# A two-block transformer kernel: another order in the first stage, in cross attention, in the queue of weight loads, and one bank given back earlier

## The reference, cut to what matters

```python
# first block
h = x
proj = rmsnorm(h, g_mix) @ w_in                     # rq rk rv rg fq fk fv ff
h = h + concat(silu(rg) * head_group_norm(retention(rq, rk, rv)),
               forgetting_attention(norm(fq), norm(fk), fv, ff)) @ w_out
h = h + memory_cross_attention(rmsnorm(h, g_xattn), mem, ...) @ w_xo
h = h + (silu(hn @ w_gate) * (hn @ w_up)) @ w_down  # hn = rmsnorm(h, g_ffn)
# memory_cross_attention: 4 heads of 256, 512 queries, 256 memory tokens
q = rmsnorm_per_head(hn @ w_xq); k = rmsnorm_per_head(kv[:half]); v = kv[half:]
o = softmax(q @ k.T / 16) @ v
# second block
mods = silu(c) @ w_ada + b_ada                      # 72 rows of 128 values
...                                                 # swiglu, convolution + window attention, swiglu
```

## Time and profile before

| | |
|---|---|
| median of 3 runs | 2117.18 us (2116.45 to 2119.18) |
| profiled execution: its own time | 2116.05 us |
| its span | 2114.2 us |
| TensorE busy | 2053.4 us (97%), 9844 matmuls |
| VectorE / ScalarE / GpSimd busy | 948.8 / 722.0 / 846.2 us |
| mean granted TensorE clock | 0.991 |

### The profile page before, as it was taken

How to read it: one execution, slowest core, us unless ns; L and a number is a source line. 1 busy time by engine, 2 the same in 40 slices (tenths; PEclk the granted TensorE clock), 3 DMA queues, 4 the chain that set the end, 5 groups by cost and what they waited for, 6 DMA issues and landing times.

```text
span 2114.2 us, 27008 instructions
## 1 busy us (share of the span) xinstructions
PE 2053.4 (97%) x9844; PEld 1685.6 (80%) x9844; DVE 948.8 (45%) x1247; ACT 722.0 (34%) x1092; POOL 846.2 (40%) x347
## 2 busy tenths in 40 slices
PE   7999899989999998999999999999999999999998
PEld 6787787868788877888888878888777888888886
DVE  3585864243888885432221143473543243222112
ACT  4234454243323322333222233224664343223221
POOL 3344323304454443344444434444223444444442
PEclk9999999999999999999999999999999999999998
DMA  5243212204556575223323324422222322323331
GB/s 198 80 130 119 81 61 73 87 11 140 179 189 197 190 266 200 91 90 99 94 94 100 97 83 119 132 97 90 67 64 70 99 90 90 99 92 97 100 95 64
DMA packets 66504, 233.26 MB, mean 110 GB/s; under 512 B 7552, under 2 KB 8832, under 8 KB 65920
## 3 DMA queue, kind: packets, MB, share of 16 engines
q1 hardware_dynamic: 64992, 229.54, 34.2%
q10 hardware_dynamic: 1440, 2.72, 0.4%
HBM read 224.37 MB, written 2.10 MB: 107 GB/s over the span
## 4 chain that ended last, share of the span: by engine, by line
issue 65%; POOL 29%; PE 5%; POOLq 1%; DVE 0%; ACT 0%; DVEq 0%
POOL wlo L414 29%; PE bank L1637 2%; PE bank L1639 2%; PE bank L1638 2%; POOLq L413 0%; POOLq L417 0%; DVE h L1498 0%; PE bank L1671 0%; DVE ssum L919 0%; POOLq L414 0%; PE bank L1662 0%; PE bank L1661 0%; DVE h L1016 0%; DVEq L123 0%; ACT tmp L494 0%
## 5 line engine op out<-in xcount | busy, mean ns | idle before, releaser
L414 POOL TENSOR_TENSOR wlo<-raw,whi 128x1024 fp32r<-128x1024 f32 x343 | 846.0, 2467 | 1245.3 <-ACT whi L440 1245.1
L1539 PE MATMUL bank<-xh,whi 128*128 128x512 f32 x1664 | 651.6, 392 | 2.3 <-ACT whi L440 1.1
L1540 PE MATMUL bank<-xl,whi 128*128 128x512 f32 x1664 | 647.7, 389 | 0.0
L440 ACT ACTIVATE whi<-raw 128x1024 fp32r<-128x1024 f32 x343 | 362.3, 1056 | 660.1 <-PE bank L1545 358.9
L1545 PE MATMUL bank<-xh,wlo 128*128 128x512 f32 x1664 | 411.2, 389 | 0.0
L1539 PEld LDWEIGHTS bank<-xh,whi 128*128 128x128 f32 x1664 | 312.4, 188 | 69.7 <-ACT whi L440 1.9
L1545 PEld LDWEIGHTS bank<-xh,wlo 128*128 128x128 f32 x1664 | 312.4, 188 | 65.1
L1540 PEld LDWEIGHTS bank<-xl,whi 128*128 128x128 f32 x1664 | 312.5, 188 | 64.3 <-issue 0.5
L1637 PE MATMUL bank<-hh,whi 128*128 (+1 forms) x528 | 206.9, 392 | 7.3 <-POOL wlo L414 7.2
L1638 PE MATMUL bank<-hl,whi 128*128 (+1 forms) x528 | 206.4, 391 | 0.0
L1639 PE MATMUL bank<-hh,wlo 128*128 (+1 forms) x528 | 206.3, 391 | 0.0
(11 more groups left out here) (273 smaller groups left out, 2157.0 us busy)
## 6 DMA issues: line engine op xcount, KB each, us to landing
raw<-units SPq DMA_DIRECT2D x343, 512.0 KB, 3.5
ada_w<-ada_rows SPq DMA_DIRECT2D x72, 512.0 KB, 4.5
h<-x_t SPq DMA_DIRECT2D x8, 256.0 KB, 6.7
dec<-decays ACTq DMA_DIRECT2D x8, 256.0 KB, 2.9
out_t<-h SPq DMA_DIRECT2D x8, 256.0 KB, 2.1
mem_in<-mem_t SPq DMA_DIRECT2D x1, 1024.0 KB, 12.7
turned_q<-proj SPq DMA_DIRECT2D x4, 256.0 KB, 5.7
turned_k<-proj SPq DMA_DIRECT2D x4, 256.0 KB, 4.1
```

The lines of the kernel that those rows point to most:

```text
L414: pool.tensor_tensor(wlo[:, j % 2 * UNIT:(j % 2 + 1) * UNIT], raw[:, j * UNIT:(j + 1) * UNIT], whi[:, j % 2 * UNIT:(j % 2 + 1) * UNIT].bit ...
L440: act.activation(whi[:, v % 2 * UNIT:(v % 2 + 1) * UNIT], raw[:, slot * UNIT:(slot + 1) * UNIT], ACT.Copy).then_inc(hi_ready, 1)
L1539: mm(bank[:, 0:n], wh, chunk(rhs[0], t, n), start=t == 0, stop=False)
L1540: mm(bank[:, 0:n], wh, chunk(rhs[1], t, n), start=False, stop=False)
```

## The change

First stage: x chunk 0 is loaded ahead of unit 0, and `csilu` moves from ACT's queue to the end of SP's first loads. ACT makes the high parts of x and units 0 and 1 first, and all squares after them; DVE makes all low parts, then itself the low parts of units 0 and 1, then the sums. POOL starts with unit 2. TensorE runs all high passes of the two units, the second two tiles behind the first, and then both low passes. Group norm: the root of the last variance goes to `xn` instead of back into bank 6, and TensorE waits for the root only. Cross attention: a second pair of banks for scores, the last `xq` unit cut around the scores of head 0, scores two heads ahead at the start, the second pair of norms between, and tiles of `xo` between the last heads. Rows: the last eight modulation rows come two units later.

```diff
-XAT_NORM_BANKS = (4, 5, 2, 5)
+XAT_NORM_BANKS = (4, 5, 0, 1)
+XAT_SCORE_BANKS = ((0, 1), (2, 5))
...
+            load_x((0,))
             load_unit(0, 0, True)
-            load_x((0, 1))
+            load_x((1, 2))
             load_unit(1, 1, True)
-            load_x(range(2, C))
+            load_x(range(3, C))
...
+            sp.dma_start(csilu[:, :], c_rows).then_inc(c_in, 16)
...
-                    if rows < (64 if u < half + 3 else NMOD * C):
+                    if rows < (64 if u < half + 5 else NMOD * C):
...
-            with pool.Fori(0, UNITS // 4) as i:
+            pool.wait_ge(lo_ready, 2)
+            for v in (2, 3):
+                low_part(v, v)
+            with pool.Fori(1, UNITS // 4) as i:
                 for j in range(4):
                     low_part(4 * i + j, j)
...
-            act.dma_start(csilu[:, :], c_rows).then_inc(c_in, 16)
+            def mix_high(c):
+                act.wait_ge(x_loaded[c], 16)
+                act.activation(chunk(xh, c), chunk(h, c), ACT.Copy, scale=col("g_mix", c)).then_inc(norm_hi, 1)
+            act.wait_ge(setup_done, 1)
+            act.activation(rs[0:32, 0:1], lt[0:32, 0:1].bitcast(f32), ACT.Copy)
+            act.wait_ge(vec_in, 16)
+            mix_high(0)
             high_part(0, 0, 0)
-            act.wait_ge(vec_in, 16)
+            mix_high(1)
+            mix_high(2)
+            high_part(0, 0, 1)
+            for c in range(3, C):
+                mix_high(c)
             for c in range(C):
-                act.wait_ge(x_loaded[c], 16)
-                norm_chunk("mix", c, c % 4, dst=xh, gain="g_mix")
-                if c == 0:
-                    high_part(0, 0, 1)
+                norm_chunk("mix", c, c % 4)
             high_part(0, 0, 2)
+            high_part(0, 0, 3)
             norm_root_of("mix")
-            high_part(0, 0, 3)
             norm_r_copy("mix")
...
-                act.activation(bank[:, :], bank[:, :], ACT.Sqrt, bias=col("eps")).then_inc(gn_root, 1)
+                if p == 3:
+                    act.wait_ge(gn_t, 3)
+                act.activation(bank[:, :] if p < 3 else chunk(xn, 0), bank[:, :], ACT.Sqrt, bias=col("eps")).then_inc(gn_root, 1)
...
                 act.wait_ge(qn_sum, pair + 1)
-                act.activation(qroot[:, 8 * pair:8 * pair + 8], banks[6 + pair][:, 0:8], ACT.Sqrt,
+                act.activation(qroot[:, 8 * pair:8 * pair + 8], banks[(6, 0)[pair]][:, 0:8], ACT.Sqrt,
                                bias=col("eps")).then_inc(qn_root, 1)
...
+            def memory_exps(hd):
+                act.wait_ge(xat.s_negmax, hd + 1)
+                if hd >= 2:
+                    act.wait_ge(xat.s_tr, hd - 1)
+                for q, b, o, w, po in XAT_GROUPS:
+                    act.activation(xat.p[hd % 2][:, po:po + w], banks[XAT_SCORE_BANKS[hd % 2][b]][:, o:o + w], ACT.Exp,
+                                   bias=nm[:, 4 * hd + q:4 * hd + q + 1], scale=xat.scale,
+                                   accum_out=sm[:, 4 * hd + q:4 * hd + q + 1]).then_inc(xat.s_exp, 1)
+            def memory_probabilities_copy(hd):
+                act.wait_ge(xat.s_tr, hd + 1)
+                if hd >= 1:
+                    act.wait_ge(xat.s_pv, hd)
+                act.activation(xat.pt[:, 0:T], banks[3][:, :], ACT.Copy).then_inc(xat.s_pt_act, 1)
+            def memory_out_high(hd):
                 act.wait_ge(xat.s_pv, hd + 1)
                 for d in range(2):
                     act.activation(chunk(yh, 2 * hd + d), banks[6 + d][:, :], ACT.Copy).then_inc(xat.s_hi, 1)
-            attention(xat, xat_evac, later_roots, copy_first=True)
+            query_squares(1, range(3), lambda c: (qn_sum, 1))
+            memory_exps(0)
+            query_squares(1, (3,), None)
+            high_part(L["xo"].u0, 0, 1)
+            memory_probabilities_copy(0)
+            memory_exps(1)
+            query_roots(1)
+            memory_out_high(0)
+            memory_probabilities_copy(1)
+            memory_exps(2)
+            memory_out_high(1)
+            memory_probabilities_copy(2)
+            memory_exps(3)
+            memory_out_high(2)
+            memory_probabilities_copy(3)
+            memory_out_high(3)
...
-                norm_chunk("mix", c, dst=(xh, xl), gain="g_mix")
+                low_chunk("mix", c, h, T, (xh, xl), "g_mix")
+            for u in range(2):
+                dve.wait_ge(hi_ready, u + 1)
+                tt(wlo[:, u * UNIT:(u + 1) * UNIT], raw[:, u * UNIT:(u + 1) * UNIT],
+                   whi[:, u * UNIT:(u + 1) * UNIT].bitcast(f32), ALU.subtract).then_inc(lo_ready, 1)
+            for c in range(C):
+                norm_chunk("mix", c)
...
-                dve.reciprocal(chunk(xn, 0), banks[5 if p < 2 else 6][:, :]).then_inc(gn_rstd, 1)
+                dve.reciprocal(chunk(xn, 0), chunk(xn, 0) if p == 3 else banks[5 if p < 2 else 6][:, :]).then_inc(gn_rstd, 1)
...
             scale_units("xq", lambda j: chunk(xq, j), last=5)
             query_square_sums(0)
             scale_units("xq", lambda j: chunk(xq, j), first=5, last=6)
             query_recips(0)
             scale_units("xq", lambda j: chunk(xq, j), first=6, last=7)
             query_norm(0)
+            query_norm(1)
+            query_square_sums(1, (0,))
+            memory_maxima(0)
             scale_units("xq", lambda j: chunk(xq, j), first=7)
-            query_norm(1)
-            query_square_sums(1)
-            def xat_evac(hd):
-                for d in range(2):
-                    c = 2 * hd + d
-                    dve.wait_ge(xat.s_hi, c + 1)
-                    tt(chunk(yl, c), banks[6 + d][:, :], chunk(yh, c).bitcast(f32), ALU.subtract).then_inc(xat.s_lo, 1)
-            attention(xat, None, xat_evac, later_recips, later_queries)
+            memory_normalise(0)
+            query_square_sums(1, (1,))
+            memory_probabilities_copy(0)
+            memory_maxima(1)
+            memory_normalise(1)
+            query_recips(1)
+            query_norm(2)
+            query_norm(3)
+            memory_probabilities_copy(1)
+            memory_out_low(0)
+            memory_maxima(2)
+            memory_normalise(2)
+            memory_out_low(1)
+            memory_maxima(3)
+            memory_probabilities_copy(2)
+            memory_normalise(3)
+            memory_probabilities_copy(3)
+            memory_out_low(2)
+            memory_out_low(3)
...
+            def opening_units():
+                for t in range(C + 2):
+                    for m, k in ((0, t), (1, t - 2)):
+                        if 0 <= k < C:
+                            if k == 0:
+                                take(m)
+                                pe.wait_ge(hi_ready, m + 1)
+                            pe.wait_ge(norm_lo, k + 1)
+                            high_passes(m, (k,), banks[m], X, T)
+                for m in range(2):
+                    pe.wait_ge(lo_ready, m + 1)
+                    low_pass(m, banks[m], X, T).then_inc(unit_used, 1)
+            opening_units()
             def wait_consts_then_columns():
                 pe.wait_ge(consts_in, 32)
                 norm_columns("mix")
-            dense("fq", [X], T, (sc, SCALED["fq"]), together=((norm_lo, 0), paced),
+            dense("fq", [X], T, (sc, SCALED["fq"]), begun=True,
...
-                    pe.wait_ge(gn_rstd, 4)
+                    pe.wait_ge(gn_root, 4)
...
+            def memory_scores(hd):
                 pe.wait_ge(qn_done, 2 * hd + 2)
                 for q, b, o, w, _ in XAT_GROUPS:
+                    b = XAT_SCORE_BANKS[hd % 2][b]
+                    if o == 0:
+                        take(b)
...
+                last.then_inc(xat.s_scores, 1)
+                for b in XAT_SCORE_BANKS[hd % 2]:
+                    bank_free[b] = [(xat.s_exp, 4 * hd + 4)]
...
+                pe.wait_ge(xat.s_pn, 4 * hd + 4)
+                take(3)
+                take(4)
...
+                pe.wait_ge(xat.s_pt_act, hd + 1)
+                pe.wait_ge(xat.s_pt_dve, hd + 1)
+                take(6)
+                take(7)
...
+                last.then_inc(xat.s_pv, 1)
+                bank_free[6] = bank_free[7] = [(xat.s_lo, 2 * hd + 2)]
...
+            dense("xq", [Y], T, (sc, SCALED["xq"]), together=((norm_lo, HI_BASE["xattn"]), sum(held(7), [])), hooks=hooks,
+                  hold_last=True)
+            last_query = L["xq"].u0 + C - 1
+            half_unit(last_query, last_query % 2, banks[3], Y, T, 0)
+            pe.wait_ge(kmem_done, C)
+            pe.wait_ge(vmem_copied, C)
+            memory_scores(0)
+            half_unit(last_query, last_query % 2, banks[3], Y, T, 1)
+            memory_scores(1)
+            memory_transposes(0)
+            query_columns(1)
+            memory_values(0)
+            query_spread(1)
+            memory_transposes(1)
+            memory_scores(2)
+            memory_values(1)
+            memory_scores(3)
+            memory_transposes(2)
```

(27 more changed lines are left out.)

86 lines of the change are left out of this document (42 added, 44 removed).

## The result

The changed kernel takes 2093.97 us in the median of four runs (2092.98 to 2095.66), the kernel before 2117.27 (2116.45 to 2119.18): a ratio of 0.9894 with a 95% interval of 0.9881 to 0.9906. Forecast were 2092.9 and a range of 2088.5 to 2101. The profiled execution took 2094.07, with a span of 2092.3.

A forecast was written before the change was run, and what follows sets the result against it. TensorE bounds the kernel, busy 2053.4 of 2114.2 us; idle and half-clock time can be won. Gains of 5.2 + 1.7 + 9.6 + 7.8 = 24.3 give 2092.9 us from the median of 2117.18; range 2088.5 to 2101.

The forecast's parts named there:

- First stage, forecast 5.2: First stage: it ends at 21.1 instead of 26.4, gain taken as 5.2 us; bounds 2.8 and 6.5.
- My cover of 1.8 us for the columns: First stage: DVE's six additions end at 19.3, under low passes that end at 21.1, so `norm_columns` need not wait.
- Group norm, forecast 1.7: Forgetting attention's first values: no longer behind DVE's reciprocal, the chain moves by 1.7 us; bounds 0.8 and 2.5.
- Cross attention, forecast 9.6: Cross attention: 5.5 us of waits, 2.8 of half clock and 1.3 of drained pipelines go; bounds 5.5 and 11.7.
- The step on the columns: Cross attention: columns wait 0.9 us for DVE's second sum, queued behind the normalisation and slowed beside POOL.
- eight places at 0.2: Cross attention: pipelines drained between stages, about 0.2 us at each of eight places that now run on, entered as 1.3.
- Rows, forecast 7.8: Down projection: the 5.4 us wait goes and 2.4 of half clock with it; bounds 5.0 and 8.2.
- such shifts: Whole kernel: other half-clock spells may shift the time by 2 us, allowed for in the range.
- A: Rival: the waits go but the clock still falls at all three places, 2100.5 us; chance 0.11.
- B: Rival: in cross attention one late step in ACT's and DVE's in-order queues delays the next head, 2098 us; chance 0.06.
- C: Rival: in the rows, unit 129 or 130 takes over the wait, half of 7.8 lost, 2097 us; chance 0.04.
- D: Rival, slower: cross attention's short groups with small waits keep the clock low, 2128 us; chance 0.02.

The follow-up runs named there:

- p_gn: The kernel before with only the group norm edit (last root out of its bank, into `xn`): 2112.91 us, ratio 0.9986.
- a_nocut: The changed kernel with the last `xq` unit run whole ahead of the scores of head 0, not cut around them: 2093.78 us.
- a_gn2: The changed kernel with DVE's last group norm reciprocal and its scaling one head later, the low part of pair 2 ahead of both: 2099.73 us in one run.
- a_rows4: The changed kernel with the last modulation rows one unit later than in the kernel before, instead of two: 2093.91 us.
- a_poollow: The changed kernel with POOL instead of DVE making the low parts of units 0 and 1: 2095.09 us, ratio 0.9902.
- a_fill: The changed kernel with three tiles of the next unit instead of one between columns and spread in two otherwise unedited norms: 2087.50 us, ratio 0.9866.

## Why the prediction was right, step by step

**First stage, forecast 5.2.** 5.37 against the profile of before, by the steps that were given: unit 0's high part made TensorE start at 6.86 (6.5), the second tile at 8.33 (7.9), DVE's low parts took 1.2 each, the low passes ended with the columns at once behind them at 21.06 (21.1). Three steps were off and fell out against each other. The clock rose after nine slow matmuls and not fifteen. The splits were later than counted, so the low parts were ready at 15.2 and 16.4 (14.0 and 15.2). And the sums did not run at 0.68: each addition waits in a semaphore for the one before it on DVE, 0.79 from start to start, and they began at 16.3, so they ended at 21.0 and not at 19.3. My cover of 1.8 us for the columns was 0.1. Against what before usually takes, the gain is smaller: the five profiles of the old stage lie at 0, 0.13, 1.04, 1.10 and 1.28, and the profile that I summed from was the most expensive; the seven of the new stage have a median of 5.37, so about 4.3.

**Group norm, forecast 1.7.** Right in mechanism, and in size against the profile of before: TensorE gained 2.56 at the first values and gave 0.82 back, with the wait that the earlier trace rows had made me expect at the next hand-over. But that profile happened to have no spell behind the wait of 3.05. Three of the five profiles of the old stage have one; against their median (-1.58 in the rest of forgetting attention) the gain is 3.4, as `p_gn` measured with 3.5. The sum had no term for that spell. In after, TensorE's timeline:

```profile
261.80 0.41 PE L2003 MATMUL bank<-tab,tmp 128*128 128x128 f32 x2 [1.04 <-DVE tmp L1368]
```

**Cross attention, forecast 9.6.** 9.58. The waits named last were there in size: the spread 0.88 (0.9), values 3 0.79 (0.7), values 2 0.10 (0.2). The clock was 1.00. The step on the columns failed: no wait of 0.9 came, since DVE's second sum was not held up by POOL. I had charged this one operation 2.6, what two took in rows 8. DVE in after:

```profile
418.59 0.68 DVE L1393 TENSOR_TENSOR tmp<-tmp 128x512 f32<-128x512 f32 x1
```

The size of the spread's wait is partly luck: TensorE was there 0.7 earlier than counted, having no wait at the columns, and DVE's chain 0.6 earlier, since it started from the end of the transposes and not from the late sum. The waits are so 1.8 and not 2.7, and the idle time fell by 6.4 instead of 5.5; that made up for a smaller gain in busy time, 3.2 instead of 4.1 (2.8 for the clock and 1.3 for the pipelines, where eight places at 0.2 would have been 1.6). Here too before's profile was dear: four other profiles of the old stage take -0.27, 0.97, 0.98 and 1.00 less, nearly all of it a shorter spell. Against their median of all five, 0.97, the gain is 8.6.

**Rows, forecast 7.8.** 8.15, with no wait from unit 127 to 131. What is queued behind SP's block of rows is unit 129, as foreseen. SP in after, the answer to the earlier trace rows:

```profile
787.31 11.22 SPq L308 DMA_DIRECT2D raw<-units  x3
810.77 1.60 SPq L320 DMA_DIRECT2D ada_w<-ada_rows  x2
...
812.40 0.43 SPq L308 DMA_DIRECT2D raw<-units  x1
```

The group of three holds units 126, 127 and 128, the last issued at 798.2; unit 129 goes out at 812.40. Counted in before's time (14.9 later) that is 827.3, where unit 127 stood.

**The sum.** 24.3 was forecast. The four places gave 24.8 (5.37 + 1.74 + 9.58 + 8.15), but the profiled executions are only 22.0 apart. What is missing lies outside the four steps, in spells: 1.67 lost ahead of the first values, 1.10 and 0.55 at the two norms, and 0.6 won at the end. I had put such shifts at 2 us in the range. Taken from medians of all profiles, the terms are 4.3 + 3.4 + 8.6 + 8.1 = 24.4, against 23.3 in the runs' medians, whose interval reaches from 19.9 to 25.2. So the sum of 24.3 is good to a us, but by luck in part: the first stage and cross attention are worth 0.9 and 1.0 less than I forecast, since before's profile was dear there, and the group norm 1.7 more, since it was cheap there.

**The rivals.** A did not come at the places it named. Its mechanism is real: `a_nocut` brings one short spell back with one wait. B did not come in after; `a_gn2` shows its price, 7 us, when a long operation is put at the wrong place of DVE's queue. C did not come; `a_rows4` shows that the slack of one unit less would have left 0.75. D, by which the chain of short groups keeps the clock low, did not come at all: 53.83 us at 1.00. That is also where the rule of the Trainium skill (TensorE: Matmul & The Clock Gate, A second HAM failure mode: psum-queue depth-cycling) stops: waits of 0.10 to 0.88 us between groups did not lower the clock here. The rule of the Trainium skill on the interfaces that GpSimd and VectorE share (GPSIMD Engine Reference, Specifications) agrees with `a_poollow`: 8.38 us for seven `xl`, operations with two inputs.

What stays open: why a given execution has the spell at 247, or when the clock rises in the first stage. The runs only show that the code does not settle it. Nor is it shown that the wait for the reciprocal brings the spell at 263; it was there in three of five profiles with that wait and in none of eight without.

## What to carry to other kernels

Before a term is taken from one profile, ask how much of it is clock: where a stretch holds a half-clock spell, the same code can give 1 to 2 us more or less there, and a second profile of the kernel before is worth as much as one of the changed one. A spell that comes in some profiles behind a wait may belong to the price of that wait, though the profile in hand does not have it. Two waits of 1.6 us on TensorE behind one-column sums cost 3.8 and 3.1 us in after's trace with their spells (2.69 + 1.10, 2.50 + 0.55); two more tiles of real work took away both waits, one spell and part of the other, which was worth more per line than all of this change but the rows. And an operation that is put off in an in-order queue needs a look at what it will stand beside and ahead of there, not only at what it leaves.

## What the runs showed of the hardware that was not expected

- Identical code differs in its half-clock spells: the clock rises at 19.13 or at 16.89 us in before, and a spell of 1.6 us at 247, or at 263 behind a wait of 3.0, is there or not. Medians of the kernels still agreed within 1.5 us (2093.97 and 2092.47).
- DVE beside POOL: seven `xl`, 0.68 us each in a row alone, took 8.38 beside two low parts of POOL. An operation with one tensor and a column, four times 512 elements, took 3.31 instead of 1.28 (`a_gn2`). A two-input addition at 418.59 in after, which began 0.2 before POOL's low part, took 0.68, and the low part 2.66.
- A low part of 1024 columns takes DVE 1.2 us alone and POOL 2.36.
- A wait of 0.75 in `a_rows4` did not lower the clock, and behind one of 1.61 in `a_nocut` it fell. At the second place of `a_fill` it fell with no wait but 0.23 ahead of the one-column sums.
